# One-hots for four tokens moved to GpSimd, five row pairs moved into the gate round, last three layer norms merged

## The reference, cut to what matters

```python
q = (h @ w_q).reshape(b, s, 8, 2, 128)
scores = jnp.einsum('bshpd,hpnd->bshpn', q, sub_keys)      # 2 x 128 scores per head
top_s, top_i = lax.top_k(scores, 16)                       # then the best 16 of the 256 sums
act = jax.nn.gelu(jnp.einsum('td,ted->te', xt, u_tab[it])) # it: the expert's number
out = jnp.einsum('te,ted->td', gt * act, v_tab[it])        # gt: softmax gates
x = _layer_norm(alpha * h + out, ln2_w, ln2_b)
```

## Time and profile before

| | |
|---|---|
| median of 3 runs | 1405.58 us (1405.57 to 1406.03) |
| the profiled execution's own time | 1404.78 us |
| its span, first to last instruction | 1402.8 us |
| mean granted TensorE clock | 0.984 |

### The profile page before, as it was taken

How to read it: one execution, slowest core, us unless ns; L and a number is a source line. 1 busy time by engine, 2 the same in 40 slices (tenths; PEclk the granted TensorE clock), 3 DMA queues, 4 the chain that set the end, 5 groups by cost and what they waited for, 6 DMA issues and landing times.

```text
span 1402.8 us, 18014 instructions
## 1 busy us (share of the span) xinstructions
PE 1342.8 (96%) x6450; PEld 949.0 (68%) x6450; DVE 1088.1 (78%) x2477; ACT 385.8 (28%) x790; POOL 685.5 (49%) x548
## 2 busy tenths in 40 slices
PE   8999998979999999997999999999999999999994
PEld 6787755568888888886754445548888885444442
DVE  4837265697999999768986789869988878666668
ACT  4213200232220102027930035456654012000000
POOL 2325111377444548761056656536555565656460
PEclk9999999989999999999999999999999999999998
DMA  7321064489899999997179999989999999999993
GB/s 247 141 77 61 11 230 150 155 302 399 304 373 379 354 367 398 414 413 279 61 274 413 413 414 411 405 311 379 370 391 338 410 414 414 413 413 413 416 413 123
DMA packets 118424, 444.22 MB, mean 317 GB/s; under 512 B 11712, under 2 KB 24512, under 8 KB 101952
## 3 DMA queue, kind: packets, MB, share of 16 engines
q0 software_dynamic: 73728, 268.47, 49.5%
q1 hardware_dynamic: 44032, 173.56, 31.8%
q10 hardware_dynamic: 576, 1.05, 0.2%
HBM read 440.94 MB, written 2.10 MB: 316 GB/s over the span
## 4 chain that ended last, share of the span: by engine, by line
PE 46%; DVE 19%; DMA 16%; issue 6%; POOL 5%; ACT 4%; DVEq 2%; ACTq 1%; SPq 0%
PE ps L1540 14%; PE ps L1452 14%; DMA big<-in_peer_v_dram,idx 13%; PE ps L1469 7%; DVE y L1272 6%; DMA big<-in_peer_u_dram,idx 3%; POOL big L649 3%; PE ps L1723 2%; PE ps L1632 2%; POOL big L635 2%; ACT wr L699 2%; DVE big L1247 1%; PE ps L1653 1%; ACT wr L701 1%; PE ps L1626 1%
## 5 line engine op out<-in xcount | busy, mean ns | idle before, releaser
L635 POOL DMA_INDIRECT big<-in_peer_u_dram,idx x256 | 319.0, 1246 | 360.7 <-DVE dots L1247 273.6
L649 POOL DMA_INDIRECT big<-in_peer_v_dram,idx x256 | 305.6, 1194 | 176.7 <-DVE y L1272 121.8
L1272 DVE SCALAR_TENSOR_TENSOR y<-big,wgt,y 128x1024 f32<-128x1024 f32 x256 | 328.0, 1281 | 76.5 <-DMA big<-in_peer_v_dram,idx 72.6
L1247 DVE CUSTOM_DVE_ANT_0 big<-big,xh 128x1024 f32<-128x1024 f32 x256 | 310.8, 1216 | 46.3 <-DMA big<-in_peer_u_dram,idx 45.6
L1540 PE MATMUL ps<-big,pool_mem 128*128 128x512 f32 x496 | 217.4, 593 | 0.0
L1452 PE MATMUL ps<-xT,big 128*128 128x256 f32 x960 | 211.1, 380 | 0.0
L1452 PEld LDWEIGHTS ps<-xT,big 128*128 128x128 f32 x960 | 181.7, 190 | 24.3
L1540 PEld LDWEIGHTS ps<-big,pool_mem 128*128 128x128 f32 x496 | 93.7, 190 | 114.8 <-issue 114.8
L1540 PE MATMUL ps<-y,pool_mem 128*128 128x512 f32 x256 | 113.6, 594 | 0.0
L1540 PE MATMUL ps<-xT,pool_mem 128*128 128x512 f32 x240 | 108.9, 605 | 0.0
L1452 PE MATMUL ps<-xT,y 128*128 128x256 f32 x480 | 106.4, 380 | 0.0
(11 more groups left out here) (286 smaller groups left out, 1540.4 us busy)
## 6 DMA issues: line engine op xcount, KB each, us to landing
big<-u_pairs_dram SPq DMA_DIRECT2D x32, 1024.0 KB, 8.0
big<-v_pairs_dram SPq DMA_DIRECT2D x32, 1024.0 KB, 8.0
y<-u_pairs_dram SPq DMA_DIRECT2D x16, 1024.0 KB, 8.1
xT<-u_pairs_dram SPq DMA_DIRECT2D x16, 1024.0 KB, 8.4
y<-v_pairs_dram SPq DMA_DIRECT2D x16, 1024.0 KB, 8.0
xT<-v_pairs_dram SPq DMA_DIRECT2D x16, 1024.0 KB, 8.0
big<-in_w_in_dram SPq DMA_DIRECT2D x24, 512.0 KB, 5.7
pool_mem<-in_peer_w_q_dram SPq DMA_DIRECT2D x12, 1024.0 KB, 9.3
```

The lines of the kernel that those rows point to most:

```text
L635: nc.gpsimd.indirect_dma_start(urow[n % RING], None, peer_u2, bass.IndirectOffsetOnAxis(ap=idx[:, u, e:e + 1], axis=0)).then_inc(s_u[n % R ...
L649: nc.gpsimd.indirect_dma_start(vrow[place], None, peer_v2, bass.IndirectOffsetOnAxis(ap=idx[:, u, e:e + 1], axis=0)).then_inc(s_v[place], 16)
L1247: V.tensor_tensor_reduce(out=urow[n % RING], in0=urow[n % RING], in1=xh[:, u // PH * D:(u // PH + 1) * D], scale=1.0, scalar=0.0, op0=ALU. ...
L1272: V.scalar_tensor_tensor(acc_rows[t], vrow[place], wgt[:, u % 2, e:e + 1], acc_rows[t], ALU.mult, ALU.add).then_inc(s_vadd, 1)
```

## The change: what it does

1. Gate round: `gate_rows` no longer makes `ohj` for tokens 0 to 3. GpSimd makes them, with four `tensor_scalar` instructions per group (128 elements from `iota`, plus a pointer scalar, compared with 0), in program order among its gathers. It waits for the gate matmuls two groups back; TensorE's `gate` job waits for the new semaphore `s_ohf`.
2. The pieces, both first `first_key` and `gate_rows(0)` move ahead to row 103 (`OPENING_ROW`); the rest of the round stands at row 105; behind groups 5, 11, 17, 23 and 29 VectorE runs the row pairs 105 to 109, and GpSimd issues their successors' gathers three groups later.
3. `team_rows` starts at 138 for (1, 0) and at 168 for (1, 1).
4. `gelu(1)` moves one head ahead; `gelu(8)` from behind `team(1, 0, 12)` to behind `team(1, 0, 6)`; `gelu(10)` from behind `act(1, 13)` to behind `act(1, 9)`; `gelu(11)` from behind `act(1, 22)` to behind `act(1, 17)`. `gelu(9)` stays behind `act(1, 4)`.
5. `last_norms` makes the three last layer norms together: all statistics, one root over three columns whose steps wait on a semaphore with the wide first passes between them, then all second passes.

```diff
-ROUND_ROW = 106
+OPENING_ROW, ROUND_ROW = 103, 105
+ROWS_IN_ROUND = {5: 105, 11: 106, 17: 107, 23: 108, 29: 109}
 def team_rows(r, s):
-    first = {(0, 1): ROUND_ROW + 1, (1, 0): ROUND_ROW + 28, (1, 1): ROUND_ROW + 58}[r, s]
+    first = {(0, 1): ROUND_ROW + 1, (1, 0): ROUND_ROW + 33, (1, 1): ROUND_ROW + 63}[r, s]
...
-        if n in (2, 4, 7):
-            jobs.append(("gelu", ((2, 4, 7).index(n),), None))
+        if n in (1, 4, 7):
+            jobs.append(("gelu", ((1, 4, 7).index(n),), None))
...
-    during = {(0, 6): 3, (0, 17): 4, (0, 30): 5, (1, 4): 9, (1, 13): 10, (1, 22): 11}
+    during = {(0, 6): 3, (0, 17): 4, (0, 30): 5, (1, 4): 9, (1, 9): 10, (1, 17): 11}
-    between = {1: 7, 12: 8}
+    between = {1: 7, 6: 8}
...
+            def first_four(g):
+                if g == 0:
+                    pool.wait_ge(s_minus, 1)
+                if g >= 2:
+                    b, used_ = BANK["gate", g - 2]
+                    pool.wait_ge(full[b], used_ + 1)
+                for t in range(4):
+                    c = 8 * g + t
+                    last = nc.gpsimd.tensor_scalar(ohj[:, g % 2, 0, :, t], iota[:], minus_key[:, c:c + 1], 0.0,
+                                                   ALU.add, ALU.is_equal)
+                last.then_inc(s_ohf, 1)
+            for n in range(ROUND_ROW + RING - 2):
+                gather(n)
+            first_four(0)
+            first_four(1)
+            n = ROUND_ROW + RING - 2
+            for n in (n, n + 1):
+                gather(n)
+            for g in range(2, GROUPS):
+                first_four(g)
+                if g - 3 in ROWS_IN_ROUND:
+                    n = ROWS_IN_ROUND[g - 3] + RING
+                    gather(n)
...
             def gate_rows(n):
-                V.tensor_tensor(ohj[:, n % 2, 0:1], spread(1, n, NK)[:, 0:1], both(grid[:], NK)[:, 0:1], ALU.is_equal)
                 dve.wait_ge(s_eq, n + 1)
...
+            def last_norms():
+                parts = [(acc_rows[1], acc_rows[1])]
+                parts += [(acc[a], xh[:, (GATHERED + a) * D:(GATHERED + a + 1) * D]) for a in range(2)]
+                ...  # bn_stats of all halves, waiting s_vdone 1 to 4; three bn_aggr; steps: 12 small ones
+                for i, step in enumerate(steps):
+                    if i:
+                        dve.wait_ge(s_root, i)
+                    step().then_inc(s_root, 1)
+                    if i < 2 * n:
+                        (z, to), c = parts[i // 2], slice(i % 2 * 512, (i % 2 + 1) * 512)
+                        V.scalar_tensor_tensor(to[:, c], z[:, c], mv[:, i // 2, 0:1], lnp2[:, 0, c], ALU.subtract,
+                                               ALU.mult).then_inc(s_centred, 1)
+                ...  # then six second passes, each released to its store
...
-                if n == ROUND_ROW:
+                if n == OPENING_ROW:
                     dve.wait_ge(s_selT, 2)
                     gate_pieces()
                     first_key(0)
-                    for g in range(GROUPS):
+                    gate_rows(0)
+                    first_key(1)
+                if n == ROUND_ROW:
+                    for g in range(1, GROUPS):
                         gate_rows(g)
-                        if g:
-                            dense_weights(g - 1)
+                        dense_weights(g - 1)
                         if g + 1 < GROUPS:
                             first_key(g + 1)
+                        if g in ROWS_IN_ROUND:
+                            product_row(ROWS_IN_ROUND[g])
+                            add_row(ROWS_IN_ROUND[g] - LAG)
...
-            finish(acc_rows[1]).then_inc(s_ln2, 1)
-            fence()
-            for a in range(2):
-                dense_output(a)
+            last_norms()
...
                     pe.wait_ge(s_oh, n_ + 1)
+                    pe.wait_ge(s_ohf, n_ + 1)
```

More of the change, by code:

```diff
@@ L493, in layer @@
         s_oh, s_ohl = sem("onehots_ready"), sem("last_eight_onehots_ready")
-        s_ohq = sem("last_four_onehots_ready")
+        s_ohq, s_ohf = sem("last_four_onehots_ready"), sem("first_four_onehots_ready")
+        s_minus = sem("negated_second_keys_ready")
         s_act, s_wgtd = sem("dense_gelu_ready"), sem("dense_weights_ready")
@@ L499, in layer @@
         s_alpha, s_zout = sem("alpha_identity_ready"), sem("dense_output_ready")
+        s_root, s_centred = sem("root_step_done"), sem("centred_and_weighted")
         s_ln2, s_out = sem("output_ready"), sem("output_stored")
@@ L651, in gather_v, with gather @@
                                              ).then_inc(s_v[place], 16)
-            for n in range(ROWS + LAG):
+            def gather(n):
                 if n < ROWS:
@@ L657, in _ @@
                     gather_v(n - LAG)
+            def first_four(g):
[21 more added lines that the diff above has]
+                    gather(n)
+            for n in range(n + 1, ROWS + LAG):
+                gather(n)
         @block.scalar
@@ L847, in _ @@
                         A.activation(minus_key, selT[:, 1, :], ACT.Copy, scale=-1.0)
-                        A.drain()
+                        A.drain().then_inc(s_minus, 1)
             for t in range(GATHERED):
@@ L1348, in gated_gelu @@
                 V.tensor_tensor(x3, ps[:, b, :].rearrange("p (i n) -> p i n", i=2), x3, ALU.mult).then_inc(free[b], 1)
[L1350 to L1355, removed]
-                fence()
[L1357 to L1363, removed]
-                fence()
-                for half in range(2):
-                    c = slice(half * 512, (half + 1) * 512)
-                    V.scalar_tensor_tensor(z[half], z[half], r, lnp2[:, 1, c], ALU.mult, ALU.add).then_inc(s_zout, 1)
-                fence()
+            def last_norms():
+                parts = [(acc_rows[1], acc_rows[1])]
+                parts += [(acc[a], xh[:, (GATHERED + a) * D:(GATHERED + a + 1) * D]) for a in range(2)]
+                n = len(parts)
+                for k, (z, _) in enumerate(parts):
+                    for half in range(2):
+                        if k:
+                            dve.wait_ge(s_vdone, 2 * k + half - 1)
+                        V.bn_stats(st[:, 2 * k + half, :], z[:, half * 512:(half + 1) * 512])
+                fence()
+                for k in range(n):
+                    V.bn_aggr(mv[:, k, :], st[:, 2 * k:2 * k + 2, :].rearrange("p a b -> p (a b)"))
+                fence()
+                v, r, a, half_bits = nw[:, 0, 0:n], nw[:, 3, 0:n], nw[:, 1, 0:n], nw[:, 2, 0:n].bitcast(i32)
+                steps = [lambda: V.tensor_scalar(v, mv[:, 0:n, 1], EPS, None, ALU.add),
+                         lambda: V.tensor_scalar(half_bits, v.bitcast(i32), 1, None, ALU.logical_shift_right),
+                         lambda: V.tensor_scalar(r.bitcast(i32), half_bits, -1.0, float(0x5F3759DF), ALU.mult, ALU.add)]
+                for _ in range(3):
+                    steps += [lambda: V.tensor_tensor(a, r, r, ALU.mult),
+                              lambda: V.scalar_tensor_tensor(a, a, -0.5, v, ALU.mult, ALU.mult),
+                              lambda: V.scalar_tensor_tensor(r, a, 1.5, r, ALU.add, ALU.mult)]
+                for i, step in enumerate(steps):
[6 more added lines that the diff above has]
+                                               ALU.mult).then_inc(s_centred, 1)
+                dve.wait_ge(s_root, len(steps))
+                dve.wait_ge(s_centred, 2 * n)
+                for i in range(2 * n):
+                    to, c = parts[i // 2][1], slice(i % 2 * 512, (i % 2 + 1) * 512)
+                    V.scalar_tensor_tensor(to[:, c], to[:, c], r[:, i // 2:i // 2 + 1], lnp2[:, 1, c], ALU.mult,
+                                           ALU.add).then_inc(s_zout if i > 1 else s_ln2, 1)
@@ L1423, in _ @@
                     reciprocal_sum(ahead_unit)
+                if n in ROWS_IN_ROUND.values():
+                    continue
                 if FIRST_ROWS <= n < ROWS:
```

## The result

The changed kernel took 1468.26 us (median of 4 runs, 1464.61 to 1472.44), the kernel before 1405.57 beside it: the ratio is 1.045, with a 95% interval of 1.042 to 1.048. Forecast were 1407.9 us. The profiled execution took 1464.61 us with a span of 1462.4, against 1404.78 and 1402.8 before, 59.6 us of span more.

The account below looks back on a forecast made before the run. TensorE, busy 96% of the span, was taken as the bound, with pauses and VectorE's tail. -0.8 - 5.7 + 12.8 - 4.0 = +2.3 us on the median 1405.58 gave 1407.9 us, range 1400.5 to 1418.

Parts of the forecast that it names:

- The round: Gate round with GpSimd one-hots and row pairs: -0.8 us, between -5.2 and +8.
- I take 0.30, 1.2 per group: Price of one GpSimd one-hot instruction in the gate round: 0.30 us, four per group; ends 0.2 and 0.9 each.
- a GpSimd instruction over 0.4 us: Sign in the changed trace's gate round that would make the forecast wrong.
- rival 1: Gate round: GpSimd and VectorE exclude each other at every meeting, round 9 us later, total 1417 to 1418; chance 0.17.
- part 1: The forecast's section on the gate round, claiming -0.8 us.
- The start of the round: TensorE's matmuls of gate 0 start near 633, after the earlier opening.
- Its best case: Gate round: ScalarE's groups run on without idling and end at 702.4, 5.2 us earlier.
- The pairs: Five VectorE row pairs inside the gate round: each makes TensorE wait 0.9 us or more.
- Part 2: Job list behind the gate round: one pause goes, -5.7 us, and a new one comes, +12.8 us.
- (b): TensorE's 3.20 us wait near 943 us for a team's one-hots, plus 2.5 low clock; forecast gone, -5.7 us.
- The pause at team (1, 1, 5): Last round: one-hots come late behind gelu(9)'s exponentials; TensorE pauses 10.3 us plus 2.5 low clock, +12.8 us.
- The end: Last layer norms: VectorE finishes 11.5 us behind TensorE instead of 15.8; -4.0 us, -3 to -5.

Follow-up runs that it names:

- run 4: Kernel before plus 28 GpSimd instructions in eight forms at its start, into scratch; the change's form took 0.89 us alone, 0.78 each in succession.
- run 6: run 5 with the row pairs also out of the gate round and the teams back near their old rows; 1390.45 us, 0.989 of before.
- run 1: Changed kernel with VectorE making the first four tokens' one-hots again, GpSimd none, row pairs kept in the round; 1419.12 us, 1.011 of before.
- run 5: Changed kernel with VectorE making all one-hots, gelu(9) at team 2 of the last round, parameter rows loaded earlier, row pairs kept; 1397.36 us, 0.995 of before.
- run 7: Changed kernel with GpSimd's one-hots kept, row pairs out of the round, teams back near their old rows; 1420.22 us, measured once.
- run 8: run 7 with GpSimd making one-hots of two tokens per group instead of four, VectorE the other two; 1392.2 us, measured once.
- Run 9: run 1 with only the two parameter rows of the second layer norm loaded earlier; 1409.68 us, 1.004 of before.
- run 10: run 1 with only gelu(9) moved from team 4 to team 2 of the last round; 1409.65 us, 1.003 of before.
- run 2: Kernel before with only the end changed, the last three layer norms worked out together; 1398.55 us against 1403.49, 0.996.

## Why the prediction was wrong, step by step

**The round, forecast -0.8, measured +46.1.** The failed step is "I take 0.30, 1.2 per group; the ends are 0.2 each ... and 0.9". The price is 0.78 each with nothing beside it (run 4), 3.12 per group. The prediction had itself named a GpSimd instruction over 0.4 us as a sign that it was wrong. Four kernels are the corners of one square, here by the time from the first gate matmul to the experts:

| | no pairs in the round | five pairs |
|---|---|---|
| VectorE makes the one-hots | 70.66 (run 6) | 78.35 (run 1), 77.36 (run 5) |
| GpSimd makes them | 100.46 (run 7) | 122.52 (the changed kernel) |

GpSimd's price alone costs 29.8 us: 30 groups at 3.12 in place of about 2.1. The pairs alone cost 7. Both together cost 51.9, 15 more than their sum, because on a full GpSimd everything that holds it up counts. From 100.46 to 122.52 it is 22.1, and GpSimd's timeline has all of it. Four pairs of gathers between lots take 2.3 us each (661.42 to 663.73), 9.3 together; the prediction had them at 3.1 each. And VectorE's row pairs hold GpSimd up: the five lots of the changed kernel, 28, 24, 24, 24 and 20 instructions in 24.82, 21.32, 21.32, 21.70 and 18.02 us, are 107.2 us where run 7 made the same 120 in 94.45. That is 12.7 us, some 2.5 for the one row pair that lies beside each lot.

The upper end of the price, 0.9, was the right value, and it was not carried through. Four times 0.9 is 3.6 us per group, against the 1.67 of VectorE and the 2.0 of ScalarE; over 30 groups that is 108 us of GpSimd in a round of 67, and it needed no new row. The text sized the bad case by the exclusion of the two engines instead (rival 1: +8 in part 1, and 9 later in the rival's own sum) and so closed its range at 1418. Rival 1's mechanism is in the runs, but elsewhere than it was put: for the round's short instructions it is 0.09 us on an `ohi` and 0.2 on a GpSimd instruction, with no effect on the round (run 8); for a row pair, with two SBUF inputs of 1024 elements, it is GpSimd that stands, for the 2.5 us above. The Trainium skill, SBUF — State Buffer, § Who interferes with whom, has the loser block for the whole instruction. The pair at 648.69 agrees: GpSimd's two instructions took 3.77 us where two take 1.6, and VectorE's took 1.22 and 1.30. The short meetings cost less than either instruction takes, and no row here shows how often they met.

The Trainium skill, GPSIMD Engine Reference, § 3.1, gives 1.8 cycles per element at best, the estimate of 0.19 us for 128 elements that stood in the prediction. Run 4 has 0.72 to 0.89 us for them, 3.3 to 4.6 ns an element and 0.3 us fixed: the Trainium skill's figure and the measurement differ, and the measurement decides.

**The start of the round** was right: forecast near 633, measured 632.71. A wait of 2.47 us for ScalarE's half of group 0 follows it, which the text did not name; the runs without GpSimd's one-hots have it too. **Its best case** was right as well: forecast 5.2 us earlier if nothing but ScalarE bounds it, run 6 has 4.5, with VectorE making the one-hots. **The pairs** were forecast at 0.9 us of waiting or more each; run 1 has 1.66 to 1.98 each, and four slower matmuls behind most.

**Part 2, the pause at team (1, 0, 15), forecast gone, -5.7.** The exponentials' wait of the earlier trace rows did go, but a pause of 9.78 us came two teams earlier. The failed step is "the pause of (b) goes": the layer norm at row 160 was looked at only for what stands behind it. It needs two parameter rows that SP loads behind 68 pairs of weights, each of which waits for TensorE to free its place. Counted from the experts' start, VectorE came to row 160 after 224.6 us in the kernel before, after 215.0 in runs 7 and 8, and after 199.0 in the changed kernel, while the second parameter row was issued at 207.6 in run 7 and at 207.2 in the changed kernel. So two things brought VectorE there early. The first is the 9.30 us that it no longer stands: then it waits about 5 us for the rows, as runs 7 and 8 show, and that costs TensorE nothing. The second is the five row pairs done in the round, with the teams moved four rows on: 16 us more of lead, a wait of 16.17, and 9.78 of it reaches TensorE. The gain of `gelu(8)` by itself was forecast well: from the experts to TensorE's end 675.4 us before, 670.3 in runs 7 and 8, 5.1 less against 5.7. The prediction did place the layer norm at team 12; what it left out is when the layer norm's parameters arrive. Run 9 takes this pause away, run 10 keeps it.

**The pause at team (1, 1, 5)**, which no trace had shown, was right: 10.3 us forecast, 10.25 measured, with VectorE 15.17 us at the exponentials; run 10 puts it at 12.0 with its low clock, against 12.8. Runs 7 and 8, whose teams stand at the old rows with `gelu(9)` unmoved, don't have it, as the prediction's order of the queues says. No run moves the teams alone, with the pairs left in the round.

**The end** was right: 11.5 us behind TensorE forecast, 10.9 measured; VectorE's end moved by -4.9 against TensorE's, the end of the span by -4.8, run 2's time by -4.9, against -4.0.

## What to carry to other kernels

Give an operation whose price no row shows both ends of its price, and multiply each through by count and by what the engine does per period; when the high end exceeds the period of the loop, that is the range's end, however unlikely the end looks. Work goes to an idle engine only at a rate: one instruction in a short loop that is longer than the loop's slack costs its excess every time, while half of them cost nothing (run 8). When a stall is taken out, follow every queue that the stalled instruction's successors depend on, the DMA queue above all: the stall may have been what made a late load punctual. And when one engine's work is moved by some rows against a fixed list of another's, look again at everything that stood between the two: here both pauses behind the round are gone without any mend once the pairs and the four rows are taken back (runs 7 and 8).

## What the runs showed of the hardware that was not expected

- GpSimd's `tensor_scalar`, f32 to f16: about 0.3 us fixed and 3.3 to 4.6 ns per element of a partition; 32 elements 0.45, 128 0.72 to 0.89, 512 2.00 us. Its `tensor_tensor` subtract on 512 elements took 1.04 us, half of the `tensor_scalar` of the same size with two operations. A select of 128 elements took 0.29 and is no measure for either.
- A write with a stride of 4 f16 elements made the 128-element form 0.89 in place of 0.72.
- GpSimd and VectorE slowed each other by 0.1 to 0.2 us an instruction where both were short (run 8). A VectorE row pair held GpSimd for about 2.5 us. GpSimd's form 4 took 1.40 at the median beside VectorE's two-input adds, 0.82 at its shortest, while the adds stayed at 1.23 each (3.68 for three).
- The list of waits can name an instruction that wrote the tile's other buffer, here the next group's `ohi`: with GpSimd the full engine (60.0 of 60 us) it put 26.5 us to VectorE and 2.7 to GpSimd. The busy times of the stretch showed the bound, the list did not.
